# 32 tokens instead of 16 gathered four partitions each, 352 dense ones, value slabs handled in pairs

## What is computed

```python
def peer_ffn(h, w_q, sub_keys, u, v):          # 128 x 128 experts, 8 heads, the best 16 of each
    ...
        q = (xc @ w_q).reshape(PEER_CHUNK, PEER_HEADS, 2, PEER_DQ // 2)
        sc = jnp.einsum('chpd,hpkd->chpk', q, sub_keys)
        top_s, top_i = lax.top_k(sc, K)
        cand = top_s[:, :, 0, :, None] + top_s[:, :, 1, None, :]
        best_s, best_flat = lax.top_k(cand.reshape(PEER_CHUNK, PEER_HEADS, K * K), K)
        ...
        expert = ia * PEER_NKEYS + ib
        g = jax.nn.softmax(best_s, axis=-1)
        a = jax.nn.gelu(jnp.einsum('cd,chkd->chk', xc, u[expert]), approximate=False) * g
        return jnp.einsum('chk,chkd->cd', a, v[expert])
```

## Time and profile before

| | |
|---|---|
| median of 3 runs | 1685.6 us (1685.28 to 1688.26) |
| profiled execution, its own time | 1683.52 us |
| its span, first to last instruction | 1681.3 us |
| TensorE busy | 1633.2 us (97%) |
| VectorE busy | 1341.1 us (80%) |
| ScalarE busy | 735.2 us (44%) |
| GpSimd busy | 455.5 us (27%) |
| bytes moved by the DMA engines | 438.47 MB, 261 GB/s over the span |

### The profile page before, as it was taken

One profiled execution on the slowest core, in us unless ns is written; L12 is line 12 of the kernel. 1 busy time (PEld: TensorE's weight loads), 2 busy tenths in 40 slices (PEclk: granted clock), 3 DMA queues, 4 the chain that ended last, 5 costly groups with the idle time before them and its releaser, 6 DMA issues. The chain is left out here.

```text
span 1681.3 us, 26829 instructions
## 1 busy us (share of the span) xinstructions
PE 1633.2 (97%) x9808; PEld 1509.0 (90%) x9808; DVE 1341.1 (80%) x2856; ACT 735.2 (44%) x1288; POOL 455.5 (27%) x314
## 2 busy tenths in 40 slices
PE   5999999999799999999999999999999999999996
PEld 4897776678688899999999999999999999999996
DVE  4534455646568899999999989768899999899898
ACT  3314444443253344667666754444333333333331
POOL 0000000000001023333133342333554555457540
PEclk9999999999899999999999999999999999999998
DMA  4461111023234478899899999999999999999991
GB/s 147 121 198 57 42 50 39 13 84 95 85 99 148 134 251 302 275 353 327 276 311 346 331 347 320 368 406 362 405 404 407 407 409 407 407 407 406 407 404 77
DMA packets 185441, 438.47 MB, mean 261 GB/s; under 512 B 17832, under 2 KB 102000, under 8 KB 182880
## 3 DMA queue, kind: packets, MB, share of 16 engines
q1 hardware_dynamic: 73872, 227.43, 37.1%
q0 software_dynamic: 44080, 161.06, 26.0%
q10 hardware_dynamic: 67360, 48.28, 8.7%
HBM read 380.57 MB, written 56.13 MB: 260 GB/s over the span
## 5 line engine op out<-in xcount | busy, mean ns | idle before, releaser
L469 PE MATMUL psS<-hT_lo,hi 128*128 128x368 f32 (+2 forms) x1464 | 503.1, 344 | 4.6 <-DVE hT_lo L1033 3.9
L460 DVE TENSOR_TENSOR lo<-raw,hi 128x1024 fp32r<-128x1024 f32 x323 | 394.4, 1222 | 132.8 <-ACT hi L456 124.8
L470 PE MATMUL psS<-hT_hi,lo 128*128 128x368 f32 (+2 forms) x1464 | 495.0, 338 | 0.0
L471 PE MATMUL psS<-hT_hi,hi 128*128 128x368 f32 (+2 forms) x1464 | 492.8, 337 | 0.0
L456 ACT ACTIVATE hi<-raw 128x1024 fp32r<-128x1024 f32 x323 | 339.8, 1053 | 160.5 <-PE psS L471 104.0
L578 POOL DMA_INDIRECT gat<-in_u_rows,idx x144 | 216.4, 1503 | 395.9 <-DVE gat L1207 214.6
L469 PEld LDWEIGHTS psS<-hT_lo,hi 128*128 128x128 f32 x1464 | 275.2, 188 | 28.7 <-issue 15.8
L471 PEld LDWEIGHTS psS<-hT_hi,hi 128*128 128x128 f32 x1464 | 275.5, 188 | 12.4
L470 PEld LDWEIGHTS psS<-hT_hi,lo 128*128 128x128 f32 x1464 | 275.2, 188 | 10.1
L578 POOL DMA_INDIRECT gat<-in_v_exp,idx x144 | 222.4, 1544 | 225.5 <-DVE gat L1207 141.6
L773 ACT ACTIVATE act_hi<-act_t 128x368 fp32r<-128x368 f32 x128 | 65.6, 513 | 275.9 <-DVE act_t L1258 265.0
(11 more groups left out here) (314 smaller groups left out, 2667.4 us busy)
## 6 DMA issues: line engine op xcount, KB each, us to landing
raw<-in_u_exp SPq DMA_DIRECT2D x128, 512.0 KB
raw<-in_v_exp SPq DMA_DIRECT2D x128, 512.0 KB
gelu_dram<-gelu ACTq DMA_DIRECT2D x128, 184.0 KB
gates_dram<-gates ACTq DMA_DIRECT2D x92, 256.0 KB
gel_in<-gelu_dram SPq DMA_DIRECT2D x128, 184.0 KB
raw<-in_w_merge SPq DMA_DIRECT2D x24, 512.0 KB
gate_even<-gates_dram SPq DMA_DIRECT2D x8, 1472.0 KB
gate_odd<-gates_dram SPq DMA_DIRECT2D x8, 1472.0 KB
```

What stands on the lines that cost most here:

```text
L460: nc.vector.tensor_tensor(lo[:, n % RING, :], raw[:, n % RING, :], hi[:, n % RING, :].bitcast(F32), ALU.subtract).then_inc(lo_done, 1)
L469: nc.tensor.matmul(out_ap, w_h, x_l, start=start, stop=False)
L470: nc.tensor.matmul(out_ap, w_l, x_h, start=False, stop=False)
L471: return nc.tensor.matmul(out_ap, w_h, x_h, start=False, stop=stop)
```

## The change

`EXTRA` goes from 16 to 32. `PARTS` becomes 4, `MORE` 32, `COLUMNS` 160, `DENSE` 352. There are 320 items instead of 288, and 44 gate batches instead of 46. The order of items (`ITEMS`) is written for the new counts, and the planner's costs are changed (TensorE's scaled with `DENSE`, VectorE's for a value slab 0.92 instead of 1.02). Gelu is laid out in DRAM so that two slabs of a partition lie next to each other and is fetched two slabs at a time, and `act_t`, `act_hi` and `act_lo` are computed for two slabs in one operation (704 columns), every second step.

```diff
@@ -54,7 +54,7 @@
 FIRST_U = FIRST_PQ + N_PQ
 FIRST_V = FIRST_U + NKEYS
 UNITS = 2 * NBLK * HEADS
-EXTRA = 16
+EXTRA = 32
 PARTS = P // EXTRA
 DENSE = SEQ - P - EXTRA
 LAST = FIRST_V + NKEYS
@@ -75,7 +75,7 @@
 
 DECODE = [4, 16, 48, 84]
 TURN = [None, 21, 57, 93]
-BATCH_AT = [23 + 2 * b for b in range(16)] + [59 + 2 * b for b in range(16)] + [95 + b for b in range(14)]
+BATCH_AT = [23 + 2 * b for b in range(16)] + [59 + 2 * b for b in range(16)] + [95 + b for b in range(12)]
 LOW_BY_ACT = 32
 GATE_AT = [at + (3 if b < LOW_BY_ACT else 2) for b, at in enumerate(BATCH_AT)]
 
@@ -94,8 +94,9 @@
          [it for j in range(HALF_SLOTS) for it in ((DOT, HALF_SLOTS + j), (AXPY, j))] +
          [it for j in range(MORE) for it in ((DOT, SLOTS + j), (AXPY, HALF_SLOTS + j))] +
          [(AXPY, HALF_SLOTS + MORE + j) for j in range(8)] +
-         [it for j in range(MORE) for it in ((AXPY, HALF_SLOTS + MORE + 8 + j), (AXPY, SLOTS + j))] +
-         [(AXPY, j) for j in range(HALF_SLOTS + 2 * MORE + 8, SLOTS)])
+         [it for j in range(HALF_SLOTS - MORE - 8)
+          for it in ((AXPY, HALF_SLOTS + MORE + 8 + j), (AXPY, SLOTS + j))] +
+         [(AXPY, SLOTS + j) for j in range(HALF_SLOTS - MORE - 8, MORE)])
 DOTS_DONE = [max(i + 1 for i, it in enumerate(ITEMS) if it == (DOT, j)) for j in range(COLUMNS)]
 COEF = 16
 
@@ -111,12 +112,12 @@
     for at in DECODE:
         for part, cost in enumerate((2.8, 4.2, 4.2, 1.0)):
             vector[at + part] += cost
-    tensor = [3.98] * (2 * NKEYS)
+    tensor = [3.98 * DENSE / 368] * (2 * NKEYS)
     for at in BATCH_AT:
         vector[at] += 2.55 if at > TURN[-1] else 1.85
         tensor[at + 3] += 0.95
     for s in range(NKEYS - AHEAD, 2 * NKEYS - AHEAD):
-        vector[s] += 1.02
+        vector[s] += 0.92
     for at in TURN[1:]:
         vector[at + 1] += 0.7
     share = 0.98
@@ -373,7 +374,7 @@
         w_dram = nc.dram_tensor("w_dram", [P, HEADS, 3 * P], F32).ap()
         c_dram = nc.dram_tensor("c_dram", [HEADS, COLS], F32).ap()
         sc_dram = nc.dram_tensor("sc_dram", [NBLK, P, 2 * HEADS * NKEYS], F32).ap()
-        gelu_dram = nc.dram_tensor("gelu_dram", [NKEYS, P, DENSE], F32).ap()
+        gelu_dram = nc.dram_tensor("gelu_dram", [NKEYS // 2, P, 2, DENSE], F32).ap()
         gates_dram = nc.dram_tensor("gates_dram", [NKEYS // VGROUP, P, STORES, VGROUP * STORED], F32).ap()
         idx_dram = nc.dram_tensor("idx_dram", [EXTRA, SLOTS], U32).ap()
         g_dram = nc.dram_tensor("g_dram", [EXTRA, SLOTS], F32).ap()
@@ -412,7 +413,7 @@
         more_out, more_idx_in, more_g_in = sem("more_out"), sem("more_idx_in"), sem("more_g_in")
         repeated = sem("repeated")
         gates_out = [sem(f"gates_out{r}") for r in range(2)]
-        gel_in_s, gate_in_s = [sem(f"gel_in{r}") for r in range(RING)], [sem(f"gate_in{r}") for r in range(2)]
+        gel_in_s, gate_in_s = [sem(f"gel_in{r}") for r in range(2)], [sem(f"gate_in{r}") for r in range(2)]
         act_done, ahi_done, alo_done = sem("act_done"), sem("ahi_done"), sem("alo_done")
         row_turned, row_done = sem("row_turned"), sem("row_done")
         gat_in, item_done, coef_done = [sem(f"gat_in{r}") for r in range(GATHERS)], sem("item_done"), sem("coef_done")
@@ -529,11 +530,12 @@
                     elif g >= 2:
                         sp.wait_ge(act_done, VGROUP * (g - 1))
                     sp.dma_start(gate_in[g % 2][:, :, :], gates_dram[g]).then_inc(gate_in_s[g % 2], 16)
-                if 0 <= v < NKEYS:
-                    sp.wait_ge(gelu_out[v % RING], 16 * (v // RING + 1))
+                if 0 <= v < NKEYS and v % 2 == 0:
+                    for w in (v, v + 1):
+                        sp.wait_ge(gelu_out[w % RING], 16 * (w // RING + 1))
                     if v >= RING:
-                        sp.wait_ge(act_done, v - RING + 1)
-                    sp.dma_start(gel_in[:, v % RING, :], gelu_dram[v]).then_inc(gel_in_s[v % RING], 16)
+                        sp.wait_ge(act_done, v - RING + 2)
+                    sp.dma_start(gel_in[:, v % RING:v % RING + 2, :], gelu_dram[v // 2]).then_inc(gel_in_s[v // 2 % 2], 16)
                 if v == 20:
                     sp.wait_ge(slab_used, FIRST_V)
                     sp.dma_start(gain_shift[:, :, :].rearrange("p r d -> p (r d)"),
@@ -765,12 +767,13 @@
             evacuated_batches = stored_parts = gelu_chunks = 0
             for s in range(2 * NKEYS):
                 v = s - NKEYS
-                if v + AHEAD >= 0 and v + AHEAD < NKEYS:
+                if 0 <= v + AHEAD < NKEYS and (v + AHEAD) % 2 == 0:
                     w = v + AHEAD
-                    act.wait_ge(act_done, w + 1)
+                    act.wait_ge(act_done, w + 2)
                     if w >= RING:
-                        act.wait_ge(slab_used, FIRST_V + w - RING + 1)
-                    nc.scalar.activation(act_hi[:, w % RING, :], act_t[:, w % RING, :], ACT.Copy).then_inc(ahi_done, 1)
+                        act.wait_ge(slab_used, FIRST_V + w - RING + 2)
+                    nc.scalar.activation(act_hi[:, w % RING:w % RING + 2, :], act_t[:, w % RING:w % RING + 2, :],
+                                         ACT.Copy).then_inc(ahi_done, 2)
                 if s < NKEYS:
                     act.wait_ge(slab_used, FIRST_U + s + 1)
                     if s >= RING:
@@ -780,7 +783,7 @@
                     split_hi(act, FIRST_U + s + RING)
                 if s < NKEYS:
                     act.wait_ge(gelu_done, s + 1)
-                    act.dma_start(gelu_dram[s], gelu[:, s % RING, :]).then_inc(gelu_out[s % RING], 16)
+                    act.dma_start(gelu_dram[s // 2][:, s % 2, :], gelu[:, s % RING, :]).then_inc(gelu_out[s % RING], 16)
                 if s == 1:
                     rows_of_first_block()
                 if s in DECODE:
@@ -1242,29 +1245,31 @@
                 v = s - NKEYS
                 if s + AHEAD < 2 * NKEYS:
                     split_lo(dve, FIRST_U + s + AHEAD)
-                if 0 <= v + AHEAD < NKEYS:
+                if 0 <= v + AHEAD < NKEYS and (v + AHEAD) % 2 == 0:
                     w = v + AHEAD
-                    g = w // VGROUP
+                    g, two = w // VGROUP, slice(w % RING, w % RING + 2)
                     if w == 0:
                         dve.wait_ge(G_mm, BATCHES)
                         dve.wait_ge(gates_out[0], 16 * STORE_PARTS * stores_of[0])
-                    dve.wait_ge(gel_in_s[w % RING], 16 * (w // RING + 1))
+                    dve.wait_ge(gel_in_s[w // 2 % 2], 16 * (w // RING + 1))
                     if w % VGROUP == 0:
                         dve.wait_ge(gate_in_s[g % 2], 16 * (g // 2 + 1))
                     if w >= RING:
-                        dve.wait_ge(ahi_done, w - RING + 1)
-                        dve.wait_ge(alo_done, w - RING + 1)
+                        dve.wait_ge(ahi_done, w - RING + 2)
+                        dve.wait_ge(alo_done, w - RING + 2)
                     at = w % VGROUP * STORED
-                    V.tensor_tensor(act_t[:, w % RING, :].rearrange("p (q t) -> p q t", t=STORED),
-                                    gel_in[:, w % RING, :].rearrange("p (q t) -> p q t", t=STORED),
-                                    gate_in[g % 2][:, :, at:at + STORED], ALU.mult).then_inc(act_done, 1)
-                if 0 <= v + 2 < NKEYS:
+                    V.tensor_tensor(act_t[:, two, :].rearrange("p s (q t) -> p s q t", t=STORED),
+                                    gel_in[:, two, :].rearrange("p s (q t) -> p s q t", t=STORED),
+                                    gate_in[g % 2][:, :, at:at + 2 * STORED].rearrange("p q (s t) -> p s q t", t=STORED),
+                                    ALU.mult).then_inc(act_done, 2)
+                if 0 <= v + 2 < NKEYS and v % 2 == 0:
                     w = v + 2
-                    dve.wait_ge(ahi_done, w + 1)
+                    two = slice(w % RING, w % RING + 2)
+                    dve.wait_ge(ahi_done, w + 2)
                     if w >= RING:
-                        dve.wait_ge(slab_used, FIRST_V + w - RING + 1)
-                    V.tensor_tensor(act_lo[:, w % RING, :], act_t[:, w % RING, :], act_hi[:, w % RING, :].bitcast(F32),
-                                    ALU.subtract).then_inc(alo_done, 1)
+                        dve.wait_ge(slab_used, FIRST_V + w - RING + 2)
+                    V.tensor_tensor(act_lo[:, two, :], act_t[:, two, :], act_hi[:, two, :].bitcast(F32),
+                                    ALU.subtract).then_inc(alo_done, 2)
                 at_position(FIRST_U + s)
                 for t, at in enumerate(DECODE):
                     if s == at:
```

## The result

The changed kernel takes 1699.25 us (median of 4 runs, 1697.75 to 1701.59), the kernel before 1686.07 (4 runs): ratio 1.0079, 95% interval 1.0067 to 1.0092, **13.2 us slower**. The forecast was 1684, its range ended at 1698, so the time lies just above it. The profiled execution took 1701.59 us.

A forecast was written before the change was run, and what follows sets the result against it. VectorE was taken as a bound just under TensorE on the up side, the DMA engines as the value side's bound. Up side -16.1 plus value side +14.2 gave -1.9 us: 1684 us, no change, range 1669 to 1698.

The forecast's parts named there:

- The pitch of 160.5 ns: Expert part's matmuls: 352 columns should take 160.5 ns, against 167.7 ns for 368, making a slab 0.173 us shorter.
- The value side bound by the DMA engines: Slabs 128 to 255: DMA engines set the pace at 407 GB/s; more gathered bytes make it 14.2 us longer, bounds +9 and +19.
- The rival in which the DMA engines are not at their limit: Value side: above 407 GB/s possible, so TensorE and VectorE limit it at about 3.9 us a slab; 1647 us, chance 0.08.
- where I had -4: Value side: the wider gelu fetch takes packets away, saving 4 us, between estimates of 1.9 and 6.2.
- I let 5.5 us of it be eaten. 354.4 - 5.5 = 348.9: Slabs 16 to 95: VectorE sets the pace, but 5.5 us of its 7.0 us lead absorbs added items; -7.1 us.
- TensorE's saving stands: Slabs 0 to 15: VectorE has 6 us free for one more item, so TensorE's full saving counts, -2.8 us.
- I read 1.00 in every stretch: Expert part's stretches: the granted clock is 1.00 in every one, so nothing hides behind TensorE's offered 44 us.
- 78.0 - 6.0 + 1.2 = 73.2: Slabs 96 to 111: VectorE, the bound, loses two gate batches of 3.0 us and gains an item; gain 4.7 us.
- ScalarE. Nothing: ScalarE, busy for 157 us of 426.9: its pairs cost nothing, at most 0.3 us where VectorE has no lead.
- VectorE keeps the whole up side: Up side: lead gone, slabs 16 to 95 gain 1.6 instead of 7.1, decode costs 2.5 more; 1692 us, chance 0.30.
- my signs of being wrong: Value side below 515 us, rate above 415 GB/s, or TensorE's up-side gaps absent or over 15 us.
- 0.16 us a slab: Value side, VectorE: saving of a merged pair by operation durations, beside 0.09 from start times; said to change nothing in the sum.

The follow-up runs named there:

- e1: Changed kernel with 16 gathered tokens, 368 dense columns, items and batches as before; only the two-slab gelu and activation pairs stay: 1682.12 us, ratio 0.9976.
- e5: Changed kernel without its 32 added items (288 in all); 352 dense columns and pairs stay: 1669.20 us.
- e4: Changed kernel with the items' VectorE operations on 512 of 1024 columns, all bytes still fetched: 1677.83 us.
- e6: Changed kernel with every gathered row after the first seven items cut to 512 of 1024 columns, VectorE operations unchanged: 1664.39 us.
- e7: Changed kernel with the up side's 109 items at the steps of the kernel before, the 12 others moved to the value side: 1701.18 us, ratio 1.0086.
- e9: Changed kernel with 12 to 14 unused filler matmuls ahead of gate batches 13, 29, 34 and the first turned keys: 1700.18 us, ratio 1.0094.
- e12: Changed kernel with the 128 transfers of gelu to DRAM issued by SP instead of ScalarE: 1705.28 us, ratio 1.0125.
- e10: Changed kernel with the up side's items as before but none in steps 95 to 106, those 11 moved to the value side: 1715.24 us.
- e3: Changed kernel with only 64 of 128 partitions gathered in every item but the first seven, VectorE's work kept: 1782.14 us.

## Why the prediction was wrong

**The sum in measured terms.** From e1, e5 and the changed kernel, in profiled times: pairs -2 (medians: -4.3), 352 columns -12.3, the 32 items +32.4 (up +15.8, value +17.0, about 1.0 us an item).

**Right.** The pitch of 160.5 ns. The value side bound by the DMA engines: +15.7 against +14.2 forecast, 182.83 MB in 446.6 us against 181.83 in 443.2, the rate 409 GB/s; e4 and e6 show that bytes and not VectorE set it. The wider operation starts its successor after 0.80 us against 0.81. The rival in which the DMA engines are not at their limit is ruled out. In part the value side's number was luck. The pairs gave -3.2 where I had -4. From e1 to e5 it changed by +1.9, where the narrower transfers and the few items that differ come to about -4 in my sum. The last 18 items cost +17.0, where 1.3 us each is 23. The terms were off by up to 6 us, in opposite directions.

**The step that failed: "I let 5.5 us of it be eaten. 354.4 - 5.5 = 348.9".** Slabs 16 to 95 took 357.0 us, a microsecond more than before. I set VectorE's summed work over 80 slabs against TensorE's and let the lead of `lo` buffer the difference. The sum is not wrong (VectorE's busy share is 97% there), but the lead was already spoken for. At the decode bursts 7 us of VectorE's work come in one piece, and the burst of step 48 alone takes 8.0 us of the lead (11.0 at slab 48, 3.0 at slab 54 before). The added items had brought it down to 2.9 at slab 48. So both users behind the burst came too late: the gate batch, which goes VectorE, ScalarE (2.48 us), TensorE, stopped TensorE for 2.74 us, and the lo part of slab 54 for 1.74 more. I had shown for the burst of step 16 alone. That the added items make these stops is shown by e7 (items of before, both stretches back within 1 us of the floor) and e4.

**A second step: "TensorE's saving stands", in slabs 0 to 15, and the same saving in slabs 16 to 31.** At slab 21 TensorE waits for the turned keys, behind a chain of VectorE's decode. It waited 1.78 us before and 3.94 in the changed kernel. It waited 3.49 to 3.98 in e4, e5 and e7 too: with half the vector work of the items, without the added items, and with the items of before. The keys came at about the time of before (TensorE goes on at 666.6 us before, at 666.5 to 668.3 in these four), and a TensorE that is there sooner waits longer. Slabs 0 to 31 take 136.6 us, as before, where TensorE offers 5.5. The items are not the main cause here.

**The clock.** I read 1.00 in every stretch and concluded that nothing hides there. In the changed kernel it fell to 1.2 GHz at the gaps, but with these gaps filled and the clock at 1.00 the up side took 568.6 us in place of 568.2 (e9). It is a sign of the stops and no term of the sum.

**Slabs 96 to 111: +4.3 in place of -4.7.** "78.0 - 6.0 + 1.2 = 73.2" averages VectorE's work over 16 slabs. The 12 slabs with batches need 1.14 + 3.0 + 1.17 = 5.3 us of VectorE each, where TensorE needs 4.82, and the four others have nothing to give back to them: 12 x 5.3 + 4 x 3.85 = 79.0. The same count with 14 batches gives 82.3 for the kernel before, which took 78.0: it had lead to spend there, 10.0 us at slab 96 and 3.0 at slab 112, and the changed kernel came with 6.0. e7 measured 79.3, e12 78.7, and e10 without items has its batches 4.8 us apart. The other 3 us are ScalarE held in its issues, as far as e12 shows it, in which other stretches changed too. My line "ScalarE. Nothing" was wrong in that: its share of busy time does not count issuing. The trace of before has the same held issues (5.21 us at 989.1), hidden by a lead that the changed kernel no longer has.

**The two sides could be added.** e4 took 20.8 us from the up side and 3.3 from the value side, and the profiled time fell by 23.8. e7 moved 12 items, and each cost 1.2 us on either side.

**The rival that came true** is "VectorE keeps the whole up side": its condition, a lead at slab 48 below 6 us, was met with 2.9, and its two terms give +0.9 for slabs 16 to 95, where +1.0 was measured. It gave 1692 because it kept the forecast's -4.7 for slabs 96 to 111 and -2.8 for slabs 0 to 15. Of my signs of being wrong, TensorE's gaps on the up side came to 17 us, over the 15 that I had called a lead that carries nothing.

**A slip in the working.** The 0.16 us a slab that I put beside my 0.09 is the merge alone at 352 columns, while my 0.09 has the narrower columns in it. By the durations of the traces the like figure is 0.20: two operations of 0.54 us a slab before, one of 0.88 after. It changes nothing in the sum.

**Open.** Why 2.74 us of idle time bring the clock down and 3.94 at 664.3 do not, where in e4 to e7 a gap of 3.5 to 4.0 us at the same place did, and why the 3.10 of e9 at 808 do not. What limits the number of transfers that ScalarE can issue ahead. Why an item costs 1.0 us on the value side from e5 to the changed kernel and 1.2 in e7.

## What to carry to other kernels

Where a buffer of lead is to carry more work, read the lead ahead of every burst and behind it, not at one place: what a burst takes is not free for anything else. Follow every chain from the filling engine to the waiting one. Cut stretches so small that the work in them is uniform: a mean over 12 loaded and 4 free steps is not a pace. Time saved on one engine ahead of a wait for another is waited for there (slab 21, e9); count it only behind the last such wait. A lower clock in the profile is not yet a cost: fill the gap and see whether the time moves.

## What the runs showed of the hardware

- **Short gaps bring the clock down, and that need not cost time.** At gaps of 2.13 to 3.52 us in a stream that was otherwise dense, the granted clock went to 1.2 GHz for 3.4 or 6.8 us, eight times in the changed kernel between 800 and 1660 us. Matmuls ahead of the gap's end that did no useful work prevented it in the three places of the up side (e9); the up side took 568.6 us in place of 568.2.
- **Gathering on the first 64 partitions alone slowed all transfers**: 268 GB/s at full share, packets of both queues at about 220 ns in place of 150 (e3). The Trainium skill (DMA: Bandwidth & Descriptors, "The descriptor swizzle") has engines 0 to 7 of a transfer to 128 partitions write partitions 0 to 63 and engines 8 to 15 the others. No row here says which engine wrote where, so this is not settled.
- **An engine that issues a transfer can be held for 5 to 7 us** while the DMA engines are full: 6.72 and 5.40 us, and two issues in a row for 9.17 at 1077.0, in the changed kernel, against 0.33 at most places.
- **Fewer, larger packets raised the rate a little**: from 407 to 411 GB/s with the pairs alone (e1).
